# The first input projection of a diffusion block computed by halves of the contraction, and its second weight block loaded ahead of the gates' blocks

## What is computed

```
mod = (silu_c @ ada_w[l] + ada_b[l])[:, None, :]
sh1, sc1, g1, sh2, sc2, g2 = jnp.split(mod, 6, axis=-1)
h_lat = modulate(x, sh1, sc1)            # rms_norm(x) * (1 + sc1) + sh1; the same for ctx
p = h @ w_in                             # even_mixer
q, k, v, r, zf, zb, ca, cg = jnp.split(p, ...)
u = ca * jax.nn.sigmoid(cg)              # then a depthwise convolution of 31 taps
```

## Time and profile before

| what | value |
|---|---|
| runs (3), median, lowest, highest | 1084.73, 1082.96, 1086.37 us |
| the profiled execution's own time | 1077.67 us |
| its span in the profile | 1075.8 us |
| PE busy | 971.2 us (90%) |
| DVE busy | 620.1 us (58%) |
| ACT busy | 181.9 us (17%) |
| chain that ended last | PE 70%, DMA 18%, DVE 7% |
| read from HBM | 303.81 MB |

### The profile page before, as it was taken

One profiled execution on the slowest core, in us unless ns is written; L12 is line 12 of the kernel. 1 busy time (PEld: TensorE's weight loads), 2 busy tenths in 40 slices (PEclk: granted clock), 3 DMA queues, 4 the chain that ended last, 5 costly groups with the idle time before them and its releaser, 6 DMA issues.

```text
span 1075.8 us, 19614 instructions
## 1 busy us (share of the span) xinstructions
PE 971.2 (90%) x7956; PEld 582.1 (54%) x7956; DVE 620.1 (58%) x1496; ACT 181.9 (17%) x348; POOL 92.1 (9%) x139
## 2 busy tenths in 40 slices
PE   3899999999999799999999964997997999978886
PEld 1343433447545599888978942443645554534432
DVE  1200599746924696776675525547416877755653
ACT  2200013136213300000000013324513000000001
POOL 4300000000100200000002014000010100000000
PEclk9799999998999899999999996999998899999999
DMA  9999968853021589999999989543223799999994
GB/s 340 395 406 387 385 221 316 301 209 135 5 78 67 193 320 372 411 390 393 408 389 405 426 367 371 188 156 156 79 81 118 281 364 399 398 390 413 419 428 167
DMA packets 65369, 315.34 MB, mean 293 GB/s; under 512 B 6375, under 2 KB 8007, under 8 KB 52512
## 3 DMA queue, kind: packets, MB, share of 16 engines
q1 hardware_dynamic: 52272, 283.64, 67.8%
q0 software_dynamic: 7728, 18.30, 5.0%
q10 hardware_dynamic: 5312, 12.59, 3.0%
HBM read 303.81 MB, written 17.17 MB: 298 GB/s over the span
## 4 chain that ended last, share of the span: by engine, by line
PE 70%; DMA 18%; DVE 7%; ACT 2%; issue 1%; SPq 1%; ACTq 0%; POOL 0%; PEldq 0%; DVEq 0%; POOLq 0%
PE ps L559 48%; DMA ring<-in_moe_w_gate 12%; PE ps L983 8%; PE ps L572 4%; PE ps L881 3%; DMA ring<-in_moe_w_down 2%; PE ps L1015 2%; DMA ring<-in_ada_w 2%; PE ps L1091 1%; SPq L471 1%; PE ps L1286 1%; DMA y_rows<-ar 1%; PE ps L815 1%; DMA xh<-y_rows,sm 1%; DVE ss L2367 1%
## 5 line engine op out<-in xcount | busy, mean ns | idle before, releaser
L559 PE MATMUL ps<-ring,ar 128*32 128x384 f32 (+6 forms) x3888 | 485.1, 468 | 30.9 <-DMA ring<-in_moe_w_gate 17.2
L559 PEld LDWEIGHTS ps<-ring,ar 128*32 128x32 f32 (+2 forms) x3888 | 203.0, 121 | 163.9 <-issue 94.9
L983 PE MATMUL ps<-ring,ar 128*32 128x128 f32 x1488 | 165.2, 273 | 0.0
L983 PEld LDWEIGHTS ps<-ring,ar 128*32 128x32 f32 x1488 | 162.0, 110 | 1.8
L2019 DVE STREAM_TRANSPOSE ar<-ar 32x256 f32<-32x256 f32 x304 | 132.1, 435 | 4.4 <-issue 0.2
L559 PE MATMUL ps<-xh,ring 128*128 128x512 f32 x256 | 114.3, 602 | 0.2 <-ACT xh L1353 0.2
L2055 DVE TENSOR_TENSOR ar<-ar,ps 128x384 f32<-128x384 f32 (+2 forms) x33 | 15.9, 481 | 136.8 <-PE ps L559 69.1
L559 PE MATMUL ps<-ring,xh 128*128 128x512 f32 x192 | 86.3, 606 | 1.8 <-ACT xh L1362 1.6
L559 PEld LDWEIGHTS ps<-xh,ring 128*128 128x128 f32 x256 | 48.2, 192 | 64.3 <-issue 63.4
L2180 DVE SCALAR_TENSOR_TENSOR ar<-ar,cpar 128x512 f32<-128x512 f32 x120 | 79.6, 744 | 0.0
L572 PE MATMUL ps<-ring,silu_c 128*32 128x512 f32 x384 | 51.3, 655 | 22.4 <-DMA ring<-in_ada_w 22.4
(11 more groups left out here) (333 smaller groups left out, 915.5 us busy)
## 6 DMA issues: line engine op xcount, KB each, us to landing
ring<-in_moe_w_gate SPq DMA_DIRECT2D x32, 2048.0 KB, 18.6
ring<-in_moe_w_down SPq DMA_DIRECT2D x32, 2048.0 KB, 21.7
ring<-in_moe_w_up SPq DMA_DIRECT2D x31, 2048.0 KB, 20.0
ring<-in_ada_w SPq DMA_DIRECT2D x24, 2048.0 KB, 16.7
ring<-in_even_w_in SPq DMA_DIRECT2D x5, 2048.0 KB, 20.1
y_rows<-gm POOLq DMA_DIRECT2D x17, 384.0 KB, 13.9
ring<-in_odd_w_in SPq DMA_DIRECT2D x3, 2048.0 KB, 16.2
y_rows<-ar ACTq DMA_DIRECT2D x16, 288.0 KB, 8.9
```

The lines of the kernel that those rows point to most:

```text
L559: return nc.tensor.matmul(o, l, r, start=start, stop=stop)
L983: m = nc.tensor.matmul(ps[96:128, bank, g * P:(g + 1) * P], xgT[:, p, c, 32 * g:32 * g + 32], w[:, c, 3 * P:HID], start=c == 0 and g == 0, ...
```

## The change

PE now needs only ada 0 and 2 (the first halves of shift and scale) to modulate the chunks 0 to 3 of `hT`. The conditioning is finished by halves (`first_turn`), and the four units of cg are computed in two halves of the contraction (`first_units`): chunks 0 to 3 of all units, then chunks 4 to 7. Each unit keeps a PSUM bank of its own. The loads are reordered: cg is the third block instead of the fifth, and ca is the sixth instead of the ninth, so that ada 4, 5, 6 become numbers 7, 8 and 9. From number 10 on the loads are as before. `mod_cols` and `mod_taken` now count one more, and POOL waits for `mod_cols` to reach 2, which is the second `first_turn`.

```diff
-    first = ada(0, 0, 1, 2, 3) + ein("cg")
-    freed = first + ada(0, *range(4, 12)) + ein("ca") + ada(1, 0, 1, 2) + ein("qk") + ada(1, 3, 4, 5, 6) + ein("v")
+    first = ada(0, 0, 2) + ein("cg") + ada(0, 1, 3)
+    freed = ada(0, 0, 2, 1, 3) + ein("cg") + ada(0, *range(4, 12)) + ein("ca") + ada(1, 0, 1, 2) + ein("qk") + ada(1, 3, 4, 5, 6) + ein("v")
-    loaded = first + ada(0, 4, 5, 6) + ein("ca") + ada(0, *range(7, 12)) + ein("qk") + ada(1, 0, 1, 2, 3) + ein("v")
+    loaded = first + ein("ca") + ada(0, 4, 5, 6) + ada(0, *range(7, 12)) + ein("qk") + ada(1, 0, 1, 2, 3) + ein("v")
...
+            def first_turn(h):
+                pe.wait_ge(sem("ada_added"), h + 1)
+                for c in range(4 * h, 4 * h + 4):
+                    m = mm(ps[:, 6 + h, 4 * c:4 * c + 4], modrow_of(0)[:, c * P:(c + 1) * P], cst[:, C_SEL:C_SEL + 4])
                 m.then_inc(sem("mod_cols"), 1)
...
                 for c in range(6):
-                    turned(c, c)
-                for n in range(1, 4):
-                    ada_block(0, n)
-                ada_turn(0, 6)
-                turned(6, 7)
+                    turned(c)
+                ada_block(0, 2)
+                first_turn(0)
                 pe.wait_ge(sem("mod_taken"), 1)
-                turned(7, 6)
+                turned(6)
+                first_units((0, 1), 0)
+                ada_block(0, 1)
+                ada_block(0, 3)
+                first_units((2,), 0)
+                first_turn(1)
+                first_units((3,), 0)
+                pe.wait_ge(sem("mod_taken"), 2)
+                turned(7)
+                first_units(range(4), 1)
+
+            def first_units(units, half):
+                i = at["ein", 0, "cg"]
+                if 0 in units and half == 0:
+                    arrived(pe, i)
+                for u in units:
+                    for c in range(4 * half, 4 * half + 4):
+                        if u == 0:
+                            pe.wait_ge(sem("hT0_dve" if c % 2 else "hT0_act"), c // 2 + 1)
+                        m = mm(ps[:, unit_bank(u), :], blk(i)[:, c, u * P:(u + 1) * P], hT[:, c, :], c == 0, c == KC - 1)
+                    if half:
+                        m.then_inc(sem("block_used" if u == 3 else "proj"), 1)
...
             def even_in():
-                for n in range(4):
-                    project("cg", n)
                 conv_params()
+                pe.wait_ge(sem("proj_taken_act"), 4)
                 for n in range(3):
                     ada_block(1, n)
...
                 if g == 2:
-                    pool.wait_ge(sem("mod_cols"), 1)
+                    pool.wait_ge(sem("mod_cols"), 2)
```

More of the change, by code:

```diff
@@ L299, in hybrid_dit, with unit_bank @@
         UNITS += [("r", 0), ("s", 0), ("r", 1), ("s", 1), ("r", 2), ("r", 3)]
-        UBANKS = 2
+        def unit_bank(u):
+            return u if UNITS[u][0] == "cg" else u % 2
         EB = (0, NE[0])
@@ L568, in ada_block @@
                     pe.wait_ge(sem("ada_added"), 4)
-                    pe.wait_ge(sem("mod_taken"), 2)
+                    pe.wait_ge(sem("mod_taken"), 3)
                 for c in range(KC):
@@ L581, in ada_turn @@
                 for c in range(KC):
-                    dims = modrow_of(g)[:, c * P:(c + 1) * P] if g == 0 else modrow_of(g)[:, c::KC]
-                    m = mm(ps[:, bank, w * c:w * c + w], dims, cst[:, C_SEL:C_SEL + w])
+                    m = mm(ps[:, bank, w * c:w * c + w], modrow_of(g)[:, c::KC], cst[:, C_SEL:C_SEL + w])
+                m.then_inc(sem("mod_cols"), 1)
+            def first_turn(h):
+                pe.wait_ge(sem("ada_added"), h + 1)
+                for c in range(4 * h, 4 * h + 4):
+                    m = mm(ps[:, 6 + h, 4 * c:4 * c + 4], modrow_of(0)[:, c * P:(c + 1) * P], cst[:, C_SEL:C_SEL + 4])
                 m.then_inc(sem("mod_cols"), 1)
@@ L602, in first_norm, with turned @@
                 pe.wait_ge(sem("xn0_ready"), NT)
-                def turned(c, bank):
+                def turned(c):
                     for j in range(NT):
-                        m = nc.tensor.transpose(ps[:, bank, j * P:(j + 1) * P], xn0[:, j, c * P:(c + 1) * P], ident)
+                        m = nc.tensor.transpose(ps[:, c, j * P:(j + 1) * P], xn0[:, j, c * P:(c + 1) * P], ident)
                     m.then_inc(sem("xn0_ps"), 1)
                 for c in range(6):
-                    turned(c, c)
-                for n in range(1, 4):
-                    ada_block(0, n)
-                ada_turn(0, 6)
-                turned(6, 7)
-                pe.wait_ge(sem("mod_taken"), 1)
-                turned(7, 6)
+                    turned(c)
+                ada_block(0, 2)
+                first_turn(0)
+                pe.wait_ge(sem("mod_taken"), 1)
+                turned(6)
[19 more added lines that the diff above has]
+                        m.then_inc(sem("block_used" if u == 3 else "proj"), 1)
             def odd_rows_turned(j):
@@ L700, in project @@
                 u = UNITS.index((kind, n))
[L701 to L704, removed]
+                b = unit_bank(u)
+                eng, c = taken_count(u - 2)
+                pe.wait_ge(sem("proj_taken_" + eng), c)
                 if kind == "s":
@@ L716, in project @@
                 for c in range(KC):
-                    if u == 0:
-                        pe.wait_ge(sem("hT0_dve" if c % 2 else "hT0_act"), c // 2 + 1)
                     if kind == "v":
@@ L839, in gla @@
                 turn_keys(1)
-                pe.wait_ge(sem("mod_taken"), 3)
+                pe.wait_ge(sem("mod_taken"), 4)
                 scores(1)
@@ L1328, in mod_taken @@
             def mod_taken(g, bank):
-                act.wait_ge(sem("mod_cols"), g + 1)
+                act.wait_ge(sem("mod_cols"), g + 2)
                 o, w = MOD_AT[ADA_GROUPS[g][0], (0, 1, 0)[g]][:2]
@@ L1347, in first_norm @@
                 A_(rstd[:, 0:NT], ss[:, 8:8 + NT], ACT.Sqrt).then_inc(sem("root_done"), 1)
-                act.wait_ge(sem("mod_taken"), 1)
                 for c in range(0, KC, 2):
-                    b = 7 if c == 6 else c
+                    act.wait_ge(sem("mod_taken"), 1 + c // 4)
                     act.wait_ge(sem("xn0_ps"), c + 1)
                     for r in range(2):
-                        ins = A_(hT[:, c, r * 256:(r + 1) * 256], ps[:, b, r * 256:(r + 1) * 256], ACT.Identity,
+                        ins = A_(hT[:, c, r * 256:(r + 1) * 256], ps[:, c, r * 256:(r + 1) * 256], ACT.Identity,
                                  bias=mod(0, 0, 0, c, r), scale=mod(0, 0, 1, c, r))
@@ L1466, in projected @@
                 wait_proj(act, u)
-                b = ps[:, u % UBANKS, :]
+                b = ps[:, unit_bank(u), :]
                 if kind == "cg":
@@ L1472, in projected @@
                 elif kind == "z":
-                    ins = A_(z_all[0:32, :], ps[0:32, u % UBANKS, :], ACT.Copy)
+                    ins = A_(z_all[0:32, :], ps[0:32, unit_bank(u), :], ACT.Copy)
                 elif kind == "v":
@@ L1701, in _, with ada_added @@
             V = nc.vector
-            def ada_added(g):
+            def ada_added(g, halves=(0, 1)):
                 if g == 2:
-                    dve.wait_ge(sem("mod_cols"), 1)
+                    dve.wait_ge(sem("mod_cols"), 2)
                 dve.wait_ge(sem(f"ada_bias{g}"), 32)
-                for h in range(2):
+                for h in halves:
                     dve.wait_ge(sem("block_used"), ada_last(g, h) + 1)
@@ L1724, in first_norm @@
                     V.tensor_scalar(xn0[:, j, :], x[:, j, :], rstd[:, j:j + 1], None, ALU.mult).then_inc(sem("xn0_ready"), 1)
[L1725 to L1735, removed]
+                for h in range(2):
+                    ada_added(0, (h,))
+                    dve.wait_ge(sem("mod_cols"), h + 1)
+                    V.tensor_copy(modT[:, 16 * h:16 * h + 16], ps[:, 6 + h, 16 * h:16 * h + 16]).then_inc(sem("mod_taken"), 1)
+                    dve.wait_ge(sem("mod_taken"), h + 1)
+                    for c in (4 * h + 1, 4 * h + 3):
+                        dve.wait_ge(sem("xn0_ps"), c + 1)
+                        for r in range(2):
+                            ins = V.tensor_scalar(hT[:, c, r * 256:(r + 1) * 256], ps[:, c, r * 256:(r + 1) * 256],
+                                                  mod(0, 0, 1, c, r), mod(0, 0, 0, c, r), ALU.mult, ALU.add)
+                        ins.then_inc(sem("hT0_dve"), 1)
             def modulated(l, w, j, bank):
@@ L2168, in conv @@
                         dve.wait_ge(sem("u_zero"), 1)
-                    V.tensor_tensor(u_in[:, n, :, HALO:HALO + 256], ps[:, u % UBANKS, :].rearrange("p (s t) -> p s t", s=2),
+                    V.tensor_tensor(u_in[:, n, :, HALO:HALO + 256], ps[:, unit_bank(u), :].rearrange("p (s t) -> p s t", s=2),
                                     mix[:, 4 + n, :].rearrange("p (s t) -> p s t", s=2), ALU.mult)\
@@ L2192, in conv_centred @@
                 for i in range(NPT):
```

(2 more changed lines are left out.)

## The result

Over 20 runs of each, the changed kernel takes 1087.53 us in the median (1080.02 to 1090.87) and the kernel before 1083.23 (1076.19 to 1087.79). The ratio is 1.004 with an interval of 1.0021 to 1.0059, so 2.3 to 6.4 us slower. The forecast was +2.0 us, 1086.7, within 1081 to 1090. The loss is small, 0.40% and 0.16% in the centres of the two intervals.

A forecast was written before the change was run, and what follows sets the result against it. PE bounds the kernel from 42.25 us, with saturated DMA queues deciding when blocks land. A 5.9 us gain, then 5.7 us idle for ada 6 and 2.2 us restart: +2.0 on 1084.7, 1086.7 us, range 1081.0 to 1090.0.

The forecast's parts named there:

- The place: PE at ca's first unit, 77.48 us before: whatever shifts it shifts the rest; forecast 79.5, +2.0 us.
- First halves: PE from cg at 28.9 us to the second turn: mod_cols reaches 2 at 46.9, 6.1 us later than before.
- Gain until the wait: PE behind the parameters and two ada blocks: 69.7 us against 75.6 before, worth 5.9 us.
- Landing of ada 6: Load 9 in SP's queue beside POOL's writes: lands at 75.4 us, PE idle for 5.7 us.
- two speeds: Loads of one block: 5.42 us at full speed (387 GB/s), 13.9 us beside POOL's writes (151 GB/s).
- Restart: PE at half clock behind the wait: ada 6 +1.8 us, ca's first unit +0.4, together 2.2 us.
- A: Rival, writes early and restart long: load 9 at 76.9, +3.1 to +4.9 us, about 1089; chance 0.32 (above +3.2).
- C: Rival in between: mod_cols at 47.5 to 48.6, load 9 from 74.5 to 72.7, +1 to -1 us; chance with D 0.15.
- B: Rival, writes late: with mod_cols at 49.1 PE is never idle, worth 3.7 us, 1081.0; chance 0.12.
- lands ahead of its use: Load 10, ada 7: lands at 82.3 us, ahead of its use behind ca's first unit.
- B's meeting point: mod_cols at 49.1 us: PE and ada 6 meet at 71.9, nothing idle, the clock stays.
- D: Rival, the stall is hidden: a wait further on takes up 2 us, result 0; chance with C 0.15.

The follow-up runs named there:

- the remedies: Changed kernel with ca's units put between the ada blocks, ratio 0.9934; with POOL's writes held back until qk's block is used, 0.9909; with both, 0.9934.
- the second set: 12 runs of the unedited changed kernel against the kernel before: 1086.81 us, ratio 1.0016 (0.9993 to 1.004).
- the filled kernel: Changed kernel with eight additional products between ada 5 and ada 6, written to a PSUM bank that nothing reads: 1086.35 us, ratio 1.0036.

## Why the prediction came out as it did

*The place.* One point, ca's first unit, was to carry everything. It moved by +2.56 us (forecast +2.0), and the remedies moved it and the time the same way.

*The time.* 1086.7 lies 0.8 us under the measured 1087.53, and a part of that is luck: it stands on a median of three runs, 1084.73, and 20 runs gave 1083.23. The difference, +2.0 against 4.3 in the centre, was less well met.

*First halves.* `mod_cols` reached 2 at 46.65 us (forecast 46.9). Half clock cost 1.4 us in the first 8 products (8.47 against 7.06), where I took 2.7; a start 0.3 us later (`hT`) and a wait of 0.8 us for ada 3, which landed at 40.3 instead of 39.7, took most of that back. This holds for two profiles of the unedited changed kernel; in four kernels with the same beginning the second turn ended at 48.1 us.

*Gain until the wait.* PE had done ada 5 at 68.94 (forecast 69.7), against 75.6 before: 6.7 us, forecast 5.9.

*Landing of ada 6.* 76.53 us (forecast 75.4). Load 6 landed at 45.7 instead of 45.3. By the prediction's two speeds each microsecond at full speed that is lost ahead of the writes costs 13.9 / 5.42 = 2.6 us beside them, so this is 1.0 us; `mod_cols` 0.25 us earlier costs 0.4 us more by the slope of 1.5. Load 8 was 1.3 us late already (62.8 against 61.5).

*Restart.* PE's clock was at half for all of ada 6 (3.47 us, +1.6) and back for ca's first unit (7.13). I took 2.2, so this term was 0.6 us too high. The page named in the prediction (the Trainium skill, "TensorE: Matmul & The Clock Gate", Part 1: The HAM clock gate) would give 3.47 x 0.5 = 1.7 us, an estimate; the trace agrees within 0.1 us.

*Sum.* +1.1 for the landing and -0.6 for the restart give the 0.5 us between 2.0 and 2.56. What the first set of runs has over that (4.3 us in the centre, 2.3 at the lower end) the second set doesn't have (1.7 us). I do not know whether any of it is real; 2.56 us lies in both intervals.

*Rivals.* A (load 9 at 76.9, +3.1 to +4.9) was near in the landing and missed by the short restart, 1.6 us. Only the profile decides against it; the 4.3 us of the first set would fit it. C is what the four profiles with the second turn at 48.1 us show in place of the forecast: it gives ada 6 between 74.5 and 72.7, and in the filled kernel it landed at 73.4. By the estimate above, the changed kernel is then 0.6 us ahead of before at ca's fourth unit and not 2.56 behind. So the forecast's own price was met in one of two ways in which the first halves run, and how often each occurs outside the profiles is not known. B's arithmetic on ada 6 was right and its price wrong: late enough writes were to give 3.7 us, but the run with the writes 4 us later gave nothing, since load 10 becomes late in turn. The step that failed is that load 10 "lands ahead of its use", which I had worked out for one hour of the writes and then carried to all. The prediction's own numbers show it: load 10 lands at about 82.3 us wherever the writes begin, as long as they end ahead of it, since the bytes ahead of it are the same; at B's meeting point PE asks for it at 71.9 + 1.85 + 7.06 = 80.8, and waits 1.5 us. D: up to 250 us no wait hid anything. Behind 559 us the shift between the two profiles shrinks from 12.9 to 10.0 us; whether waits for the experts' weights take up a part there was not tested.

*What I left out.* The forecast for the profile (1079.7) missed the span's 10 us, because it treated the granted clock behind 110 us as fixed. It is not, by 5 us between two profiles of the same products. It also took one way through the first halves for the only one.

## What to carry to other kernels

Loading a block earlier puts another one later: in a saturated queue follow every load behind the moved one to its use, and look at the one that the in-order engine asks for first. If a wait remains, it can be cheaper to change what the engine asks for (ca's units between the ada blocks, 7.3 us ahead at the same point) or to move a transfer that nobody waits for out of the saturated stretch (the zeros: 0.9% under before over 6 runs, 0.6 to 1.2%), than to reorder the loads. Compare kernels of this kind by one point in the program behind the change, too; their medians carry the granted clock of a thousand microseconds. That point still carries the clock ahead of it, here up to 1.8 us, so look there first when two profiles differ.

## What the runs showed of the hardware

TensorE's granted clock fell to 0.50 in stretches in which it was busy without a pause, for 3.4 us behind products with 8 columns and for 6.8 us at the end of products over 33 rows, and not in each execution. Between 110 and 160 us the mean clock was 1.00 once, 0.97 twice, 0.93 twice and 0.90 six times in eleven profiles. One unit of a projection took 8.80 instead of 7.13 us after a wait of only 1.90 us, while an ada block after 1.30 us kept full clock (1.92 us). Ada blocks took 3.10 to 3.51 us after waits of 2.39 to 2.54 us in the four kernels with the late second turn, and 3.46 and 3.47 us after 4.29 and 7.63 us. While POOL's writes ran, its queue and SP's moved 1571 packets each in 21 us, 5.52 MB against 3.15 MB.
